# Keeping half of the output projection's weights for each layer's second token block, and loading late modulation weights elsewhere

## What is computed

```
cs = silu(c)
for l in range(2):
    mod = cs @ w_ada[l] + b_ada[l]               # w_ada[l]: 1024 x 6144
    sh1, sc1, gt1, sh2, sc2, gt2 = split(mod, 6)
    h = x * (1 + sc1) + sh1
    proj = h @ w_in[l]                           # 1024 x 1440
    o = concat(mla(512), conv(256), window_attention(256))
    mix = o @ w_o[l]                             # 1024 x 1024
    x = layer_norm(alpha * x + (1 + gt1) * mix)
    h = x * (1 + sc2) + sh2
    y = peer(h, w_pq[l], sub_keys[l], u_tab[l], v_tab[l])
    x = layer_norm(alpha * x + (1 + gt2) * y)
```

## Time and profile before

| | |
|---|---|
| time, median of 3 runs | 1756.97 us (1756.77 to 1760.47) |
| span of the profiled execution | 1708.0 us |
| PE / DVE / POOL busy | 72% / 62% / 57% |
| bytes read from HBM | 664.97 MB |
| mean rate over the span | 391 GB/s |
| loads of `w_o` | 28 into `wo`, 4 into the ring, 512 KB each |

### The profile page before, as it was taken

How to read it: one execution, slowest core, us unless ns; L and a number is a source line. 1 busy time by engine, 2 the same in 40 slices (tenths; PEclk the granted TensorE clock), 3 DMA queues, 4 the chain that set the end, 5 groups by cost and what they waited for, 6 DMA issues and landing times.

```text
span 1708.0 us, 16190 instructions
## 1 busy us (share of the span) xinstructions
PE 1229.6 (72%) x5018; PEld 546.6 (32%) x5018; DVE 1062.6 (62%) x3052; ACT 413.4 (24%) x1000; POOL 981.4 (57%) x1044
## 2 busy tenths in 40 slices
PE   6988639789766577798766578798866666666564
PEld 2476413355222122254231122255322222222111
DVE  0155746577666576577566676577666686677652
ACT  1463102453210022354031022355120021001000
POOL 2000437567666566566566566566676667667763
PEclk8988859899877779899988778899987787778779
DMA  9999999999999999999999999998999999999996
GB/s 363 345 352 367 393 352 366 405 405 408 406 399 405 409 403 408 405 402 392 402 403 405 409 387 408 405 389 330 410 405 405 405 406 406 405 408 409 409 410 224
DMA packets 217190, 667.12 MB, mean 391 GB/s; under 512 B 21586, under 2 KB 50611, under 8 KB 217106
## 3 DMA queue, kind: packets, MB, share of 16 engines
q0 software_dynamic: 148240, 538.63, 80.0%
q1 hardware_dynamic: 68866, 127.46, 20.2%
HBM read 664.97 MB, written 1.05 MB: 390 GB/s over the span
## 4 chain that ended last, share of the span: by engine, by line
DMA 47%; PE 20%; DVE 14%; POOL 9%; issue 6%; ACT 3%; SPq 1%; POOLq 0%; DVEq 0%; ACTq 0%
DMA ring<-in_u_tab,uidx 22%; DMA ring<-in_v_tab,vidx 18%; PE y L1720 7%; DVE ring L1267 6%; DMA wo<-in_w_ada 5%; POOL ring L659 5%; POOL ring L671 4%; PE m L1576 2%; PE qb L1665 2%; PE m L1608 2%; SPq L505 1%; ACT rows L842 1%; PE m L1431 1%; PE m L1546 1%; DVE junk L1243 1%
## 5 line engine op out<-in xcount | busy, mean ns | idle before, releaser
L1720 PE MATMUL y<-ring,place 128*32 128x512 f32 x2048 | 627.8, 742 | 376.6 <-DMA ring<-in_v_tab,vidx 340.2
L1267 DVE SCALAR_TENSOR_TENSOR ring<-ring,hp 128x1024 f32<-128x1024 f32 x512 | 620.3, 1216 | 422.4 <-DMA ring<-in_u_tab,uidx 403.8
L659 POOL DMA_INDIRECT ring<-in_u_tab,uidx x512 | 488.0, 953 | 511.9 <-DVE ring L1267 303.5
L671 POOL DMA_INDIRECT ring<-in_v_tab,vidx x512 | 483.5, 944 | 165.6 <-issue 144.2
L1720 PEld LDWEIGHTS y<-ring,place 128*32 128x32 f32 x2048 | 126.6, 123 | 693.3 <-issue 690.3
L1665 PE MATMUL qb<-wpq,hT 128*128 128x256 f32 x512 | 138.6, 411 | 0.0
L1665 PEld LDWEIGHTS qb<-wpq,hT 128*128 128x128 f32 x512 | 97.5, 202 | 71.5 <-issue 60.2
L902 ACT ACTIVATE cdiag<-cst,wdT 128x128 f32<-128x128 f32 x248 | 79.4, 391 | 63.2 <-PE m L1608 63.1
L1431 PE MATMUL m<-win,hT 128*128 128x480 f32 x186 | 82.1, 583 | 2.6 <-ACT hT L755 2.4
L1608 PE MATMUL m<-cdiag,hc 128*128 128x128 f32 x496 | 70.8, 285 | 0.0
L957 ACT ACTIVATE gexp<-best,nbest 128x16 f32<-128x16 f32 x32 | 9.9, 308 | 249.8 <-DVE nbest L1234 249.6
(11 more groups left out here) (244 smaller groups left out, 1271.4 us busy)
## 6 DMA issues: line engine op xcount, KB each, us to landing
ring<-in_w_ada SPq DMA_DIRECT2D x34, 1024.0 KB, 13.5
wpq<-in_w_pq SPq DMA_DIRECT2D x28, 1024.0 KB, 16.5
win<-in_w_in SPq DMA_DIRECT2D x31, 720.0 KB, 14.1
wo<-in_w_ada SPq DMA_DIRECT2D x14, 1024.0 KB, 15.0
wo<-in_w_o SPq DMA_DIRECT2D x28, 512.0 KB, 9.7
ring<-in_u_tab,uidx POOLq DMA_INDIRECT x512, 13.9
ring<-in_v_tab,vidx POOLq DMA_INDIRECT x512, 14.1
ring<-in_w_o SPq DMA_DIRECT2D x4, 512.0 KB, 9.0
```

The source lines that it names most:

```text
L659: nc.gpsimd.indirect_dma_start(out=ring[:, n % UR, :], out_offset=None, in_=u_flat, in_offset=bass.IndirectOffsetOnAxis(ap=uidx[:, g % 2, ...
L671: nc.gpsimd.indirect_dma_start(out=ring[:, UR + n % VR, :], out_offset=None, in_=v_flat, in_offset=bass.IndirectOffsetOnAxis(ap=vidx[:, g ...
L1267: v.scalar_tensor_tensor(ring[:, n % UR, :], ring[:, n % UR, :], 1.0, HP[:, :], ALU.mult, ALU.mult, accum_out=dots[:, g % 2, k:k + 1]).the ...
L1720: e = mm(Y[n][lo:lo + QUAD, :], place[:, g % 2, run_of(k), :], ring[:, UR + (g * TOPK + k) % VR, n * 512:(n + 1) * 512], start=g % PH == 0 ...
```

## The change

Blocks 1 and 3 (`WO_KEPT`) start their output projection with the four chunks that the block before left in `wo`: their order is (6, 7, 4, 5, 0, 1, 2, 3), the first four steps load nothing, and SP issues only steps 4 to 7. The waits for the transposed attention and convolution outputs move to the steps that read them (`HELD_BY`). So `wo` may no longer hold modulation chunks after block 0. (1, 8), (1, 11), (0, 10) and (0, 11) go instead to `win`, in three places of 1 MB that their eight halves use in turn, so that some halves load one chunk earlier. Layer 0's chunks 10 and 11 are multiplied at slots -7 and 1 (`LATE_SLOT`) instead of -2 and 2.5. Block 1's first five input weights load after chunk 11 of layer 0 has been multiplied, at slot 1.1 instead of -62.

```diff
-WO_ORDER = (0, 1, 2, 3, 6, 7, 4, 5)
+WO_ORDERS = ((0, 1, 2, 3, 6, 7, 4, 5), (6, 7, 4, 5, 0, 1, 2, 3))
+WO_KEPT = (1, 3)
+HELD_BY = {0: "ot0", 6: "ot1", 4: "pw"}
...
+LATE_SLOT = (-7, 1)
...
-    if c < 4 or c >= 10:
-        at = BASE[0] + c if c < 4 else (-2, 2.5)[c - 10]
+    if c < 4:
+        at = BASE[0] + c
         return at, at + 0.75, at + 1.25, at + 2
+    if c >= 10:
+        at = LATE_SLOT[c - 10]
+        return at, at + 0.7, at + 1.2, at + 1.7
...
-            [view(wo, b * half_n, KC // 2, ADA_N) for b in range(2)]
+            [view(wo, b * half_n, KC // 2, ADA_N) for b in range(2)] + \
+            [view(win, b * half_n, KC // 2, ADA_N) for b in range(3)]
+
+        IN_WIN = ((1, 8), (1, 11), (0, 10), (0, 11))
...
+            if (l, c) in IN_WIN:
+                n = 2 * IN_WIN.index((l, c)) + half
+                return 8 + n % 3, n // 3 + 1
...
             def output_weights(m, slot, after):
 
                 yield slot
-                full(sp, after)
-                for j in range(WO_SLOTS):
-                    wo_load(m, j)
+                if not wo_kept(m):
+                    full(sp, after)
+                    for j in range(WO_SLOTS):
+                        wo_load(m, j)
...
+            def chunks_in_win():
+                yield -62
+                full(sp, ("sk3", 0))
+                ada_load(1, 8)
+                ada_load(1, 11, 0)
+                yield SECOND_SLOT[8] + 0.1
+                sp.wait_ge(s["mod_full"], 8 - ADDED + 1)
+                ada_load(1, 11, 1)
+                ada_load(0, 10, 0)
                 yield SECOND_SLOT[11] + 0.1
-                sp.wait_ge(s["mod_full"], ADA_CHUNKS - ADDED)
-                ada_load(0, 10)
-                yield ada_slot(10)[0] + 0.5
+                sp.wait_ge(s["mod_full"], 11 - ADDED + 1)
+                ada_load(0, 10, 1)
+                ada_load(0, 11, 0)
+                yield ada_slot(10)[0] + 0.1
                 full(sp, ("ad", 10))
-                ada_load(0, 11)
+                ada_load(0, 11, 1)
...
-                                 input_weights(1, -62, ("sk3", 0)), query_weights(),
+                                 input_weights(1, ada_slot(11)[0] + 0.1, ("ad", 11)), chunks_in_win(), query_weights(),
...
-                for j, k in enumerate(WO_ORDER):
+                for j, k in enumerate(wo_order(m)):
                     yield b + 59 + 2 * j
                     slot = wo_slot(m, j)
-                    pe.wait_ge(s[f"wo_in{slot}"], 16 * (2 * m + j // WO_SLOTS if m else 1))
+                    pe.wait_ge(s[f"wo_in{slot}"], 16 * wo_count(m, j))
                     if j == 0:
-                        taken(pe, ("ot0", m))
                         banks = [fill((f"w{n}", m)) for n in range(2)]
-                    if j == 4:
-                        taken(pe, ("ot1", m))
-                    if j == 6:
-                        taken(pe, ("pw", m))
+                    if k in HELD_BY:
+                        taken(pe, (HELD_BY[k], m))
```

More of the change, by code:

```diff
@@ L362, in build @@
         ada_places = [view(ring_all, b * half_n, KC // 2, ADA_N) for b in range(6)] + \
-            [view(wo, b * half_n, KC // 2, ADA_N) for b in range(2)]
+            [view(wo, b * half_n, KC // 2, ADA_N) for b in range(2)] + \
+            [view(win, b * half_n, KC // 2, ADA_N) for b in range(3)]
+        IN_WIN = ((1, 8), (1, 11), (0, 10), (0, 11))
         def ada_pair(c):
-            return c % 2 if c < ADDED else (2, 3, 1, 2, 3)[c - ADDED]
+            return c % 2 if c < ADDED else (2, None, 1, 2, None)[c - ADDED]
         def ada_place(l, c, half):
+            if (l, c) in IN_WIN:
+                n = 2 * IN_WIN.index((l, c)) + half
+                return 8 + n % 3, n // 3 + 1
             if l:
                 pair = ada_pair(c)
-                return pair * 2 + half, (2, 2, 3, 3)[pair] + sum(ada_pair(i) == pair for i in range(c + 1))
-            if c in (3, 7) or c >= 9:
-                return 6 + half, {3: 1, 7: 2, 9: 3, 10: 6, 11: 7}[c]
+                return pair * 2 + half, (2, 2, 3)[pair] + sum(ada_pair(i) == pair for i in range(c + 1))
+            if c in (3, 7, 9):
+                return 6 + half, {3: 1, 7: 2, 9: 3}[c]
             return ((0, 1, 2, None, 0, 1, 2, None, 2)[c] * 2 + half, (1, 1, 1, None, 2, 2, 2, None, 3)[c])
@@ L380, in wo_slot, with wo_order, wo_kept, wo_count @@
             return (j + WO_SLOTS) % KC if m == 0 else j % WO_SLOTS
+        def wo_order(m):
+            return WO_ORDERS[1 if wo_kept(m) else 0]
+        def wo_kept(m):
+            return m in WO_KEPT
+        def wo_count(m, j):
+            slot = wo_slot(m, j)
+            return sum(1 for i in range(m + 1) for q in range(KC) if wo_slot(i, q) == slot
+                       and (i, q) <= (m, j) and not (wo_kept(i) and q < WO_SLOTS))
         def sums_of(c):
@@ L427, in build @@
         names = """dve_chain act_chain consts_in c_in x_in cs_ready rows_in cols_made cols_out
-        ada_in0 ada_in1 ada_in2 ada_in3 ada_in4 ada_in5 ada_in6 ada_in7 cols_ready0 cols_ready1 sums_ready mod_full mod_rows mod_sums wo_in4 wo_in5 wo_in6 wo_in7 win_in0 win_in1 win_in2 win_in3 win_in4 win_in5 win_used small_in0 small_in1
+        ada_in0 ada_in1 ada_in2 ada_in3 ada_in4 ada_in5 ada_in6 ada_in7 ada_in8 ada_in9 ada_in10 cols_ready0 cols_ready1 sums_ready mod_full mod_rows mod_sums wo_in4 wo_in5 wo_in6 wo_in7 win_in0 win_in1 win_in2 win_in3 win_in4 win_in5 win_used small_in0 small_in1
         wo_in0 wo_in1 wo_in2 wo_in3 wo_used
@@ L519, in wo_load @@
                 slot = wo_slot(m, j)
-                sp.dma_start(wo_w[slot], w_o[m // TB, WO_ORDER[j] * P:(WO_ORDER[j] + 1) * P, :]
-                             ).then_inc(s[f"wo_in{slot}"], 16)
+                k = wo_order(m)[j]
+                sp.dma_start(wo_w[slot], w_o[m // TB, k * P:(k + 1) * P, :]).then_inc(s[f"wo_in{slot}"], 16)
             def first_output_weights():
@@ L587, in second_modulation @@
                 ada_load(1, 7)
-                ada_load(1, 8)
                 yield BASE[0] + 76.9
@@ L591, in second_modulation @@
                 ada_load(1, 9)
[L592 to L595, removed]
+                yield SECOND_SLOT[7] + 0.1
+                sp.wait_ge(s["mod_full"], 1)
+                ada_load(1, 10)
             def first_keys():
```

## The result

Over 20 runs of each, the changed kernel took 1746.94 us in the median and the kernel before 1760.09: a ratio of 0.993, 95% interval [0.991, 0.995], or 12.3 us less (9 to 16). Forecast were 1742 us and 14.9 us less. One run of the kernel before, at 1862.85 us, is left out of the ratio.

The account below looks back on a forecast made before the run. DMA bytes were taken to set the pace once gathers run. From span 1708.0, 10.4 us for bytes and 4.5 for the start leave 1693.1; with 48.97 around it, 1742 us, range 1736 to 1754.

Parts of the forecast that it names:

- The sum: Whole kernel: span 1708.0 - 10.4 - 4.5 = 1693.1 us, plus 48.97 us around it, giving 1742.1 us.
- Bytes: Blocks 1 and 3 each drop four 512 KB `w_o` loads: 4.19 MB at 405 GB/s saves 10.4 us.
- The rival that attention eats it: Block 3's saving is lost in its attention stretch; part of the only-bytes-or-less rival, gain 5 to 12 us, chance 0.27.
- The new order: Blocks 1 and 3, output projection: needing chunks 6 and 4 earlier costs no time, 0 us.
- The start: Before and early in block 1: closed hole 8.5 us minus new gap 4 gains 4.5 us; bounds 0 and 9.1.
- The closed hole: DMA lull at 250 to 270 us, 9.1 us in all, of which 8.5 us counted as closed.
- The new gap: Near 170 us, DMA runs dry because input loads leave slot -62: about 4 us lost.
- The chain: Late `w_ada` chunks come sooner: chunk 11 multiplied about 191 us, `ad10` done about 207, `ad11` about 223 instead of 249.8.
- The earlier `ad10` and `ad11`: Slots -7 and 1: multiplies ahead of other work cost 0 if halves land in time; 0 to 4 us kept.
- the second gap at 190 to 206: DMA empties again while SP waits for chunk 11; part of the only-bytes-or-less rival, gain 5 to 12 us, chance 0.27.
- The late input weights: Block 1: loads issued from 223 us, first landing 233 to 238, PE reaching slot 8 at 240; no loss.
- The slower rival: Block 1: late input weights stall PE over 33 us, resting DMA more than 14.9 us; kernel slower, chance 0.06.

Follow-up runs that it names:

- second session: Experiments on chip 14 taking the new start apart; the changed kernel rerun there measured 1689.06 us, ratio 0.9898 to the kernel before (1706.46 us).
- the start alone: Changed kernel, but blocks 1 and 3 load all eight `w_o` chunks again, so no bytes saved: 1700.95 us, ratio 0.9953 to the kernel before.
- e2_keep3_old_start: Kernel before with its old start, only block 3 keeping its four `w_o` chunks: 1702.34 us, ratio 0.9966 to the kernel before.
- the trace after: Trace of the unmodified changed kernel rerun on chip 14, span 1690.3 us; that run measured 1692.22 us, ratio 0.9905 to the kernel before.
- the first trace: First profiled execution of the unmodified changed kernel, at the lower DMA rate: 1739.82 us, span 1737.9 us.
- e3_keep1_start: Changed kernel, but block 3 loads all eight `w_o` chunks and only block 1 keeps its four: 1696.62 us, ratio 0.9934 to the kernel before.
- e5_old_late_slots: Changed kernel with layer 0's chunks 10 and 11 back at slots -2 and 2.5: 1691.71 us, ratio 0.9910 to the kernel before.
- e10_inputs_after_drain: Changed kernel with block 1's five input loads held until the last `v` gather in flight landed: 1756.59 us, ratio 0.9947 to the kernel before.

## Why the prediction was right, by its steps

**The sum (14.9 us).** It lies between the first result, 12.3 us (9 to 16), and the three later ones, 16.2, 17.4 and 17.1. The ratio of the first result and that of the second session, 0.993 and 0.9898, differ by 0.0032, more than their error of 0.0024, and nothing here tells why. The bytes and the trace's two windows add up to 10.4 + 5.9 = 16.3 us.

**Bytes (10.4 us).** Right in kind and within the error in size: 16.2 - 8.0 = 8.2 us between the start alone and the whole, error about 3.5. Block 3's part was measured twice, at 5.8 and 4.9 us, for 5.2 worked out. The rival that attention eats it is refuted by the time (`e2_keep3_old_start`) and by SP's issues behind the attention stretch. The page of the Trainium skill cited ahead, "DMA: Bandwidth & Descriptors", section Specifications, would have made it 11.7 us; the times can't tell that from 10.4, but the trace after holds 403 to 410 GB/s in most slices, so its 358 is not the limit here.

**The new order (0).** In the trace after, L1609 waits for neither the convolution's nor the attention's copy; in the first trace it waits once for a copy, for 2.4 us. The loads of `w_o` are 24 in all, as forecast.

**The start (4.5 us).** The mechanism held, and by the times the term was too small. Measured were 8.0 us (6 to 10), or 7.0 by the medians; the windows give 9.3 - 3.4 = 5.9, in the trace of the start alone 4.9, and the lead at block 1 is 5.2. The closed hole was booked at 8.5 us and measured 9.3. The new gap was booked at 4 and measured 3.4, but not quite where I had put it: 0.9 us of it lie at 140 to 150 us. There DMA runs dry in both kernels while SP waits for block 0's output projection, 7.7 us in the trace before and 8.8 in the trace after. In four more traces with the new start the wait is 8.7 to 9.2 us, but in `e3_keep1_start`, which has the same start, it is 7.7 and the window moves 332 GB/s. So whether the edit makes this part is open; without it the gap is 2.6 us and the net 6.7. The other 2 to 3 us of the timed gain arise behind block 1 (the lead is 5.2 us there, 7.2 at block 3 and 8.0 at the end) and have no cause shown; they are within the scatter of about 3 us.

**The chain.** Expected were chunk 11 of layer 1 at 191, `ad10` at 207, `ad11` at 223. Measured: 191.2, 208.3 and 221.9, the ends of the L1398 rows above. The price of 7.5 us for 1 MB beside gathers carried over from one trace to the other.

**The earlier `ad10` and `ad11` (0 to 4 us) and the second gap at 190 to 206.** PE stood 9.7 us before `ad10`, more than assumed, but DMA held 394 to 395 GB/s from 180 to 210 us, so it cost nothing. The second gap did not come.

**The late input weights.** Expected without loss; PE found them there at 248.5 us and had waited for `v` gathers instead (7.4 and 4.1 us). This slot was expected at 240: I had reckoned with 2.4 us a slot and left out that the `v` gathers behind it were just starting. The slower rival's rule, that a stall costs only once the rings have landed, was tried at 6.9 us of stall, where TensorE was no later, and at 19.7. In the second DMA stayed full through the first ten us and more, as the rule says; the price beyond the rings is open between 3.5 us and twice that.

**The step that failed** is the one that put 48.97 us around the span, where 1.7 to 1.9 lie. The trace before has the DMA rate of chip 14 and the timed runs have the times of chip 1, and what was added was the distance between the two. The forecast of 1742 us was near 1746.94 only because the timed runs, not the profiled execution, were taken as its base.

## What to carry to other kernels

When DMA is full, price an edit by two books: its bytes at the measured rate, and each time in which DMA has nothing outstanding. A stall of TensorE, even one of 10 us, took no DMA time here as long as the transfers in flight outlasted it; in the reverse case, a chain of "load, use, load the next into the same place" makes a hole as soon as the rings fill up behind it.

Half chunks in three places, instead of whole ones in one, brought `ad11` from 249.8 us to 229.8 with the slots left as they were (`e5_old_late_slots`). Whether that or the input weights in hand at 220 to 250 us closed the hole was not fully separated. `e10_inputs_after_drain` speaks for the chunks: with no input weight issued before 254 us DMA lacks 3.5 us there, against 9.3 in the kernel before.

## What was not expected of the hardware

The same kernel takes 1689 to 1692 us on chip 14 and 1748 on chip 1. The difference of 57 us is as large as three or four such changes. In the traces it is a lower DMA rate (387 instead of 406 GB/s from 1200 to 1600 us, at a DMA share of 1.00 instead of 1.03), but not an even one. This is the rate line of the first trace:

```profile
GB/s 366 367 356 340 391 410 403 406 355 372 400 405 402 405 405 406 406 360 385 400 405 393 405 405 406 406 308 349 380 389 402 388 386 387 393 369 362 382 355 246
```

Many slices hold the 400 to 410 of the other chip. The ninth is at 355 and the 27th at 308, where the trace after has 405 and 372, and behind the 27th only one holds 400. All four traces of chip 1 dip at the same places: 313 to 362 in the ninth slice, 305 to 330 in the 27th. What makes the rate drop there, and whether another run of chip 1 would be quicker, was not tried. The ratios of the changed kernel on the two chips are alike: 0.9905 and 0.9898 on chip 14, 0.9903 on chip 1; the first result's 0.993 stands somewhat apart, as said above.
